# ConvFFN of a 2-layer decoder on one core: four PSUM banks for the down projections, rounding ahead of the Gelu, norm steps moved by a tile

## What is computed

```
def conv_ffn(x, prev, w_up, conv_w, conv_b, w_down):
    up = x @ w_up                                   # 1024 -> 2 x 2816
    u, val = up[..., :D_FF], up[..., D_FF:]
    u_pad = concatenate([prev, u], axis=1)
    c = conv_b
    for j in range(3):
        c = c + conv_w[j] * u_pad[:, j:j + L]
    h = gelu(c, approximate=True) * val
    return h @ w_down, u_pad[:, -2:]                # 2816 -> 1024

h = h + rms_norm(mixer(rms_norm(h)))                # "post" and "pre" norms
h = h + rms_norm(conv_ffn(rms_norm(h)))
```

## Time and profile before

| | |
|---|---|
| median of 3 runs | 3046.87 us (3045.66 to 3049.13) |
| the profiled execution | 3053.48 us |
| its span, first to last instruction | 3051.4 us |
| TensorE busy | 2610.9 us, 86% |
| its weight loads | 2280.8 us, 75% |
| VectorE busy | 1700.0 us, 56% |
| ScalarE busy | 1089.3 us, 36% |
| GpSimd busy | 990.5 us, 32% |
| mean granted TensorE clock | 0.915 |
| DMA | 255.16 MB, 84 GB/s on average |

### The profile page before, as it was taken

The page is one execution under the profiler, slowest core; times in us unless marked ns, Lnnn a source line. Parts: engine busy times, 40 slices in busy tenths (PEclk is TensorE's granted clock), DMA queues, the critical chain, the costliest instruction groups (busy, mean ns, idle before and its releaser), DMA issues.

```text
span 3051.4 us, 37488 instructions
## 1 busy us (share of the span) xinstructions
PE 2610.9 (86%) x15437; PEld 2280.8 (75%) x15437; DVE 1700.0 (56%) x2493; ACT 1089.3 (36%) x1664; POOL 990.5 (32%) x388
## 2 busy tenths in 40 slices
PE   3777777778799999989999788777799999999995
PEld 2556676777687788889999556666677887999995
DVE  2445543544366555565665676666566544565555
ACT  2433343233344333333333444443244332423332
POOL 1232221221234544334444132212134444334341
PEclk8888887788799999999999888888899999999997
DMA  6111121221233232242322311411133232232222
GB/s 154 49 42 49 56 70 57 97 71 44 71 99 125 87 95 85 83 132 76 92 83 90 117 49 49 122 67 39 33 118 112 83 103 91 91 120 88 90 84 82
DMA packets 93799, 255.16 MB, mean 84 GB/s; under 512 B 10948, under 2 KB 44205, under 8 KB 91821
## 3 DMA queue, kind: packets, MB, share of 16 engines
q1 hardware_dynamic: 69916, 209.24, 22.2%
q10 hardware_dynamic: 23712, 43.52, 4.1%
HBM read 225.92 MB, written 26.74 MB: 83 GB/s over the span
## 4 chain that ended last, share of the span: by engine, by line
PE 64%; DVE 14%; ACT 8%; issue 7%; DMA 3%; POOL 3%; SPq 1%; ACTq 0%; DVEq 0%
PE banks L425 34%; PE banks L445 23%; ACT w_hi L407 3%; POOL w_lo L411 2%; DMA w_raw<-wall 2%; DVE normed L550 2%; PE banks L696 1%; DVE c L1292 1%; DMA normed<-h_scratch 1%; DVE acc L535 1%; DVE stats L1651 1%; DVE scores L1646 1%; DVE normed L489 1%; PE banks L752 1%; POOL act_lo L563 1%
## 5 line engine op out<-in xcount | busy, mean ns | idle before, releaser
L411 POOL TENSOR_TENSOR w_lo<-w_raw,w_hi 128x1024 fp32r<-128x1024 f32 x366 | 903.9, 2477 | 1947.3 <-ACT w_hi L407 1947.1
L425 PE MATMUL banks<-act_hi,w_lo 128*128 128x272 f32 (+1 forms) x2952 | 993.5, 337 | 48.5 <-DVE act_lo L563 30.6
L425 PE MATMUL banks<-act_lo,w_hi 128*128 128x272 f32 (+1 forms) x2952 | 977.5, 331 | 0.0
L425 PE MATMUL banks<-act_hi,w_hi 128*128 128x272 f32 (+1 forms) x2952 | 977.0, 331 | 0.0
L425 PEld LDWEIGHTS banks<-act_hi,w_lo 128*128 128x128 f32 x2952 | 576.5, 195 | 113.7 <-issue 42.3
L407 ACT ACTIVATE w_hi<-w_raw 128x1024 fp32r<-128x1024 f32 x366 | 379.8, 1053 | 643.6 <-PE banks L445 580.7
L425 PEld LDWEIGHTS banks<-act_lo,w_hi 128*128 128x128 f32 x2952 | 576.7, 195 | 43.7 <-issue 0.7
L425 PEld LDWEIGHTS banks<-act_hi,w_hi 128*128 128x128 f32 x2952 | 574.5, 195 | 45.5
L457 DVE TENSOR_TENSOR acc<-acc,banks 128x272 f32<-128x272 f32 (+1 forms) x624 | 322.7, 521 | 307.4 <-PE banks L445 307.4
L445 PE MATMUL banks<-h_hi,w_lo 128*128 128x272 f32 (+1 forms) x1056 | 362.0, 343 | 71.1 <-DVE acc L457 44.5
L445 PE MATMUL banks<-h_lo,w_hi 128*128 128x272 f32 (+1 forms) x1056 | 351.8, 333 | 0.0
(11 more groups left out here) (209 smaller groups left out, 3001.4 us busy)
## 6 DMA issues: line engine op xcount, KB each, us to landing
w_raw<-wall SPq DMA_DIRECT2D x366, 512.0 KB, 3.6
normed<-h_scratch ACTq DMA_DIRECT2D x12, 704.0 KB, 5.0
h_scratch<-acc ACTq DMA_DIRECT2D x3, 2176.0 KB, 7.3
h_scratch<-acc ACTq DMA_DIRECT2D x3, 2048.0 KB, 6.5
gstates<-state ACTq DMA_DIRECT2D x4, 1024.0 KB, 5.1
gla_s<-gstates ACTq DMA_DIRECT2D x4, 1024.0 KB, 6.6
bias<-bias_scratch SPq DMA_DIRECT2D x32, 128.0 KB, 3.4
bias_scratch<-bias_rows SPq DMA_DIRECT2D x1, 3064.0 KB, 36.6
```

What stands on the lines that cost most here:

```text
L411: nc.gpsimd.tensor_tensor(WL[:, b % RING], WR[:, b % RAW], WH[:, b % RING].bitcast(fp32), ALU.subtract).then_inc(w_lo, 1)
L425: last = nc.tensor.matmul(PS[:, bank, 0:n], w, a[X][:, k, o:o + n], start=(k == 0 and first), stop=(k == KT - 1 and w is wh and a is AH))
```

## The change

1. Down units go round four banks, 4 to 7, and wait for the unit four back.
2. On ScalarE the rounding that follows the val block stands ahead of the Gelu, and waits for the val block first.
3. The row sums of the other half (steps 2 and 6 on TensorE) stand between the u and the val block of tiles 3 and 7, where they stood behind the down groups of tiles 2 and 6. They wait until the last down group has been added.
4. Steps 2 to 8 on ScalarE and 2 to 7 on VectorE come one tile later: on VectorE the post-norm pieces at tiles 4 and 5, the folds of the pre-norm at 6 and 7, its two pieces at 8 and 9. GpSimd's act_lo pieces go behind u10 and behind d4a, where they stood behind d3a and u10.
5. In pass 1 the kv blocks stand between tile 11's u and val, the transposes between tile 13's.

```diff
@@ weight_order, ffn
             put(("u", f, 2 * g + t), bt)
+            if f == 1 and 2 * g + t == 11:
+                for x in range(2):
+                    put(("kv", 0, x), W_KV + x)
             put(("val", f, 2 * g + t), bt + 1)
...
-            if f == 1 and g == 5:
-                for x in range(2):
-                    put(("kv", 0, x), W_KV + x)
@@ pe_ffn
+        PE_STEPS, DVE_STEPS = {3: 2, 7: 6}, {1: 0, 2: 1, 4: 2, 5: 3, 6: 4, 7: 5, 8: 6, 9: 7}
+        ACT_STEPS = {0: 0, 1: 1, 3: 2, 4: 3, 5: 4, 6: 5, 7: 6, 8: 7, 9: 8}
...
                     project(pe, X, BLK["u", f, t], c, t % 2 if n == 1 else c, u_full)
+                between(t)
                 pe.wait_ge(w_lo, BLK["val", f, t] + 1)
...
-                              [HH[:, t] for t in range(2)], [HL[:, t] for t in range(2)], 4 + m % 2, 2)
+                              [HH[:, t] for t in range(2)], [HL[:, t] for t in range(2)], 4 + m % 4, 4)
+            def between(t):
+                step = PE_STEPS.get(t)
+                if step is not None and (step < 4 or f < 3):
+                    pe.wait_ge(dn_add, dn_end((f, t // 2 - 1)))
+                    pe_step(pe, *FFN_PASS[f], step, 6)
...
             for t in range(FT):
                 tile(t)
                 if t % 2 == 0 and t:
+                    if t in (4, 8) and (t == 4 or f < 3):
+                        pe.wait_ge(ms_done, NORMS[FFN_PASS[f][0], "post" if t == 4 else ("pre", "kv")[f == 1], FFN_PASS[f][1]])
+                    if f == 1 and t in (12, 14):
+                        pe.wait_ge(kv_ev, KVF[0, 1, 0])
+                        if t == 14:
+                            pe.wait_ge(kt_ev, 1)
                     downs(t // 2 - 1)
-                if t == 2 or t == 6 and f < 3:
-                    pe_step(pe, *FFN_PASS[f], t, 6)
@@ dve_ffn
-                    down_add(dve, X, (f, g), m, 4 + m % 2, g == 0)
+                    down_add(dve, X, (f, g), m, 4 + m % 4, g == 0)
...
-                if 1 <= t <= (4 if f == 3 else 8):
-                    dve_step(dve, *FFN_PASS[f], t - 1)
+                step = DVE_STEPS.get(t)
+                if step is not None and (step < 4 or f < 3):
+                    dve_step(dve, *FFN_PASS[f], step)
@@ act_ffn
+                bias(t)
...
+                act.wait_ge(val_full, TILE[f, t, n - 1])
+                round_after(act, ("val", f, t))
...
-                bias(t)
                 gelu(t)
-                act.wait_ge(val_full, TILE[f, t, n - 1])
-                round_after(act, ("val", f, t))
                 if t % 2 == 0 and t:
                     downs_done(t // 2 - 1)
                 hi(t)
-                if t <= (3 if f == 3 else 8):
-                    act_step(act, *FFN_PASS[f], t, 6)
+                step = ACT_STEPS.get(t)
+                if step is not None and (step < 4 or f < 3):
+                    act_step(act, *FFN_PASS[f], step, 6)
...
-                if f == 3 and t == 4:
+                if f == 3 and t == 5:
                     act_y_store(act, 0)
@@ POOL_LO
-        POOL_LO = {("d", 0, 3, 0): ((1, "pre", 1, 0),), ("u", 0, 10): ((1, "pre", 1, 1),),
-                   ("d", 1, 3, 0): ((2, "kv", 0, 0),), ("u", 1, 10): ((2, "kv", 0, 1),),
+        POOL_LO = {("u", 0, 10): ((1, "pre", 1, 0),), ("d", 0, 4, 0): ((1, "pre", 1, 1),),
+                   ("u", 1, 10): ((2, "kv", 0, 0),), ("d", 1, 4, 0): ((2, "kv", 0, 1),),
...
-                   ("d", 2, 3, 0): ((3, "pre", 1, 0),), ("u", 2, 10): ((3, "pre", 1, 1),)}
+                   ("u", 2, 10): ((3, "pre", 1, 0),), ("d", 2, 4, 0): ((3, "pre", 1, 1),)}
```

More of the change, by code:

```diff
@@ L1245, in downs @@
                     down_unit(pe, X, (f, g), m, [BLK["d", f, g, t] for t in range(2)],
-                              [HH[:, t] for t in range(2)], [HL[:, t] for t in range(2)], 4 + m % 2, 2)
-            for t in range(FT):
+                              [HH[:, t] for t in range(2)], [HL[:, t] for t in range(2)], 4 + m % 4, 4)
[4 more added lines that the diff above has]
+                    pe_step(pe, *FFN_PASS[f], step, 6)
                 if f == 1 and t == 11:
                     pe.wait_ge(al_done, 2 * ACTS[2, "kv", 0])
+                    pe.wait_ge(dn_add, dn_end((f, t // 2 - 1)))
                     for x in range(2):
@@ L1253, in pe_ffn @@
                         project(pe, 0, BLK["kv", 0, x], 0, 6 + x, kv_full)
-                if f == 1 and t == 12:
+                if f == 1 and t == 13:
                     pe.wait_ge(kv_ev, KVF[0, 1, 0])
+                    pe.wait_ge(dn_add, dn_end((f, t // 2 - 1)))
                     for i in range(HB):
@@ L1258, in pe_ffn @@
                     last.then_inc(kt_full, 1)
+            for t in range(FT):
                 tile(t)
                 if t % 2 == 0 and t:
+                    if t in (4, 8) and (t == 4 or f < 3):
[4 more added lines that the diff above has]
+                            pe.wait_ge(kt_ev, 1)
                     downs(t // 2 - 1)
-                if t == 2 or t == 6 and f < 3:
-                    pe_step(pe, *FFN_PASS[f], t, 6)
             downs(FG - 1)
```

## The result

The changed kernel takes 3089.43 us, median of 4 runs (3083.06 to 3095.56), against 3046.26 (3040.61 to 3049.13) of the kernel before on the same chip: ratio 1.0144, 95% interval 1.0119 to 1.0169. It is 43 us slower, where +16 was forecast and 3079 was the end of the range. Its profiled execution took 3089.86 (span 3087.7, mean granted clock 0.912).

A forecast was written before the change was run, and what follows sets the result against it. TensorE was taken to bound the kernel, waiting 60.2 us for VectorE's adds. Passes 0 and 2 +9.7 each, pass 1 +0.6, pass 3 -2.6, small terms +1 and -2: +16.4, giving 3063 us, range 3037 to 3079.

The forecast's parts named there:

- Banks four instead of two: Down groups: two more units may start, 2.8 us in passes 0 and 2, 1.5 in 1 and 3; clean stretches nothing.
- Rounding ahead of the Gelu: ScalarE: Gelu starts 1.0 to 1.5 us later in clean tiles; GpSimd's subtraction comes earlier, into VectorE's steps where VectorE is late.
- just cover: Clean down groups: first bank free after 3.1 us, four units take 3.1; 1 us lost in all.
- +2.4 us in each stalled tile: Stalled tiles, passes 0 and 2: GpSimd's subtraction lands inside VectorE's late convolution or residual; full 2.4 us taken, bound 0.
- Rival A: Faster: GpSimd's halves miss VectorE's steps, load early; passes 0 and 2 -2.6 each, total -16, 3031 us; 18%.
- tile 6: Later post-norm piece makes TensorE wait 4.4 us for a weight: +4 in passes 0 and 2, +1.5 in pass 1.
- In passes 1 and 3 ScalarE's scale step waits for VectorE first, so the subtraction comes behind it by itself: Stalled tiles of passes 1 and 3: the 2.4 us subtraction was not charged there.
- The second sum: Between tile 7's blocks: new wait 3.7 us (3.2 in pass 1); tile 8 -2.6 in passes 0 and 2, -4.2 in 1.
- Tile 10: Last norm piece at tile 9 waits for GpSimd's act_lo: +11.9 us in passes 0 and 2, +8.3 in pass 1.
- Tails and tiles 12, 14: Down groups after tile 21: -2 us in all; tiles 12 and 14 of pass 1: 1.2 gained each by the banks.
- B: No change: rival A's cases half and half, tile 10 near 5.2 to 7.3; 3041 to 3053 us, middle 3047; 22%.
- C: Slower: stalls over 3 us take the half clock, loads 8.5; 3 to 4 us more in four places, 3075 to 3085; 14%.

The follow-up runs named there:

- experiment 9: The kernel before with the down projections on four banks, norm steps unmoved and row sums in banks 4 and 5: 3017.92 us, ratio 0.991.
- experiment 4: The changed kernel with ScalarE's rounding put back behind the Gelu: 3042.52 us, ratio 0.9988.
- experiment 5: The changed kernel, rounding still ahead, but GpSimd's subtraction for a val block waits for VectorE's product of the same tile: 3058.24 us, ratio 1.0016.
- experiment 10: experiment 8 with pass 1's last norm piece also at tile 10 and pass 3's y stores one tile later: 3007.60 us, ratio 0.9874.
- experiment 2: The changed kernel with the last norm piece of passes 0 and 2 at tile 10, GpSimd's second act_lo behind u12: 3065.76 us, ratio 1.0064.
- experiment 3: The changed kernel with the down projections back on two banks: 3151.54 us, ratio 1.0358.
- experiment 8: The changed kernel with the edits of experiment 1, experiment 2 and experiment 4 together: 3007.89 us, ratio 0.9854.
- experiment 1: The changed kernel with the second row sum behind tile 7's val block instead of between its blocks: 3072.26 us, ratio 1.0085.

## Why the prediction was right in direction and wrong in size

Its sign and its largest terms held. The change splits, in the stretches, into four banks -32.4 (experiment 9 against before), the other order +21.8 (experiment 4 against 9) and the rounding +41.6 (after against experiment 4): +31.0. The pieces depend on the sequence: in the kernel before, the rounding costs 51.4 and the order 20.2.

**Banks.** "Banks four instead of two" was right as a mechanism, and tile 4 of passes 0 and 2 came out to 0.1. Alone they give 32.4; the sum never showed this, since it had them inside terms in which the two other parts filled what they freed. "In clean stretches there is nothing to win" was wrong by 0.33 us in each of those of passes 1 and 3 (experiment 9).

**Rounding ahead of the Gelu.** This is the step that failed: what GpSimd's subtraction costs in passes 1 and 3 was put at nothing. By its parts:
- For clean stretches the text had the four banks "just cover" the late product: 36.37 after, 36.50 before, 36.17 with the rounding behind. Right, but for the sign of the small term: +1 forecast, -1.3 measured.
- "+2.4 us in each stalled tile" of passes 0 and 2: right in size. A held convolution step took 2.88 in after and 0.74 in experiment 4. That VectorE cannot work on SBUF beside the subtraction is too wide, though: in before an add from a bank into acc kept its 0.69 (from 1040.02) inside a subtraction of 2.40 (from 1039.44). What was held are steps such as the convolution's, the fold and the copy of two columns. Rival A, which also had the load early, had the same order without it: -6.9 at tile 4 and 0 at tile 6, and experiment 4 shows -8.0 (43.1 to 35.1) and -0.4 (35.1 to 34.7, the wait for the weight 0.91). From A to the forecast each of these passes grows by 12.3; from experiment 4 to after they grew by 11.0 and 9.4. At tile 6, +4 forecast and +4.5 measured, two misses cancelled: the wait for the weight was 3.20 where 4.4 stood, and the clock cost 2.6 (36.40 busy, 33.81 before) where 1.2 stood. That is luck. The clock drops in the sums, 1.2 to 2.4, are estimates; what the earlier trace rows show is 36.17 busy at clock 0.92 against 33.60 at 1.00, 2.6 more.
- "In passes 1 and 3 ScalarE's scale step waits for VectorE first, so the subtraction comes behind it by itself": wrong. It comes behind the scale step, but ahead of VectorE's copies, which I had not listed between convolution and product. From A to the forecast these two passes grow by 7.6 and 1.1; from experiment 4 to after they grew by 13.3 and 7.9. Tile 6 of them came out at +4.6 and +5.4 where +1.5 and 0 stood, 8.5 of the 15 that are missing; with the rounding behind, or with GpSimd waiting for the product, it stands at 38.9 and 38.0, against 38.4 and 36.5 before. The copy ahead of tile 6's product in pass 1, in after and with the rounding behind:
```profile
1382.27 2.32 DVE L1317 COPY conv_new_t<-u 128x2 f32<-128x2 f32 x1
...
1359.06 0.16 DVE L1317 COPY conv_new_t<-u 128x2 f32<-128x2 f32 x1
```
- At tile 8 of pass 1 the adds kept TensorE for 3.28 in after and for 0.18 with the rounding behind (45.35 and 42.38, with -4.2 forecast on 46.37): 3.2 more of the 15. Experiment 5 has 44.5 there, so most of it is ScalarE's order.
- The table load of 1.28 ahead of the Gelu, which stands in a row with the rounding at tile 4 of pass 1 in experiment 5, was not in the text. Experiments 4 and 5 put all that isn't the subtraction at 9 us by the ratios and 15.6 in the stretches; what the load alone is worth was not measured.

In pass 3 a second thing stands at tile 6, which the text left out too: the four y stores keep ScalarE for 3.74 us between h_hi and the next copy. They look costly, but experiment 10 gives them 0.9 at most.
```profile
2747.47 0.66 ACT L1402 ACTIVATE h_hi<-hf 128x544 fp32r<-128x544 f32 x1 [2.43 <-DVE hf L1334]
2747.48 3.74 ACTq L1438 DMA_DIRECT2D yT<-acc  x4
2751.32 0.66 ACT L1379 ACTIVATE u<-banks 128x272 f32<-128x272 f32 x2 [3.19 <-issue]
```

**The second sum.** Forecast: a wait of 3.7, and 5.4 in place of 8.0. In pass 2 the wait was 3.6; in pass 0 it was 5.78. Passes 0 and 2 of the six kernels with the sum in this place had 3.62 three times and 5.6 to 5.8 nine times, with the rounding behind as well: the forecast had the rarer case. VectorE's fold and GpSimd's subtraction started 0.04 and 0.12 us apart, in pass 0 (first two rows) and in pass 2 (last two):
```profile
984.14 2.88 DVE L497 TENSOR_TENSOR rstd<-rstd,normed 128x544 f32<-128x544 f32 x1
...
984.10 2.35 POOL L411 TENSOR_TENSOR w_lo<-w_raw,w_hi 128x1024 fp32r<-128x1024 f32 x1 [1.90 <-ACT w_hi L407]
...
2359.73 0.72 DVE L497 TENSOR_TENSOR rstd<-rstd,normed 128x544 f32<-128x544 f32 x1
...
2359.85 2.81 POOL L411 TENSOR_TENSOR w_lo<-w_raw,w_hi 128x1024 fp32r<-128x1024 f32 x1 [2.06 <-ACT w_hi L407]
```
The clock fell with either wait: the sum itself ran at 0.50 in both, and over 6 us from its start the mean was 0.65 behind the 5.78 and 0.76 behind the 3.62. The three passes are 8.0 of the missing 15: 4.8 in passes 0 and 2 by this order, and the 3.2 of pass 1 that go with the rounding.

**Tile 10.** +11.9, +11.9, +8.3 forecast, +11.8, +11.5, +8.6 measured; the wait for the weight was 9.20 against 9.5, the clock of the stretch 0.89. Following one chain through four engines from rows of a place where the same order already stood is what made it good. Experiment 2 confirms the cause.

**Tails and tiles 12, 14.** -2 and -2.4 forecast, -4.6 and -1.2 measured; small, and of both signs.

The rivals: A (GpSimd's halves miss VectorE's steps) and B, half of it, are out by the rows of experiment 4. C came nearest in time, but only half of its reason holds. The residuals at tile 4 waited 0.29 us for a load at most, where those of the same norm piece at tile 3 had waited up to 1.72 before, so it wasn't the loads. The clock did fall in full at tile 6, but shorter waits took that back; of the missing 15, 11.7 go with the rounding. D is out by experiment 3. The range ended 10 us short because its upper end came from C alone, and the cost of the rounding in passes 1 and 3 was given no upper bound. What stays open is the 12 us between the stretches' +31.0 and the medians' +43: scatter outside the passes fits it, but isn't shown to be all of it.

## What to carry over

An instruction that releases work on another engine (here a 1.05 us rounding that starts a 2.4 us subtraction) is to be costed at every place where that work now lands, with each small instruction between it and the critical step listed by name. Cost a bundle of edits as each part alone and against the bundle without it: here one part gave 32 us, one took 42, and the sum hid both. When a term comes out well because two rows lie in a fixed order by tenths of a us, give it a second value for the other order.

## What the hardware showed that I had not expected

- Even a two-column copy on VectorE was held until GpSimd's instruction had ended, at 1341.63 against 1341.60 in pass 1 of after: 0.16 us became 2.31, and the mean of 44 such copies went from 211 to 706 ns between experiment 4 and after.
- The holding went both ways and by turns: GpSimd's 2.40 took 4.42 behind VectorE's residual, and VectorE's next step then took 2.88.
- The outcome differed between executions of equal code: tile 8 of pass 1 took 45.35 in after and 49.05 in experiment 2, whose pass 1 is the same; there the sum waited 5.22 instead of 3.05 and ran at clock 0.50 instead of 1.00.
- Four banks in turn kept the clock at 1.00 in every clean stretch of after. In its passes 0 and 1 the clock fell in ten places, each time with a wait of TensorE's own of 2.71 us or more. The length of the wait alone did not decide it: a wait of 3.05 (the sum of pass 1) and one of 2.71 (at 1562.55) left it at 1.00; tile 6 of pass 1 ran its down group at 1.00 with a wait of 1.98 (experiment 4) and at 0.89 with one of 1.99 (experiment 8). Nor does equal code with equal waits settle it: behind the same 2.85 in the same place the whole stretch had 0.96 in after and 1.00 in experiment 1 (42.94 and 41.43 us).
